# Attention slots of a decoder step: unit work ahead of the sample's work, and an earlier start of the first product

## The reference, cut to what matters

```python
z = rmsnorm(x, norm1_g) @ w_in            # q, three K/V pairs, gates, pooling input
# prompt and sample each: compressed, selected-block and window attention, merged by gates
o = g0 * o_cmp + g1 * o_sel + g2 * o_win
h = x + concat(o, pool_mix(u)) @ w_out
y = h + peer_ffn(rmsnorm(h, norm2_g))     # product-key search, single-neuron experts
```

## Time and profile before

| | us |
|---|---|
| median of three runs | 1768.33 |
| the profiled execution's own time | 1764.12 |
| its span on the core | 1762.4 |
| around the span | 1.7 |
| TensorE busy in the span | 1682.8 (95%) |
| VectorE / ScalarE / GpSimd busy | 1369.0 / 739.3 / 457.6 |
| project, attend, all later stages | 0 to 162, 162 to 397, 398 to 1762 |

### The profile page before, as it was taken

The page is one execution under the profiler, slowest core; times in us unless marked ns, Lnnn a source line. Parts: engine busy times, 40 slices in busy tenths (PEclk is TensorE's granted clock), DMA queues, the critical chain, the costliest instruction groups (busy, mean ns, idle before and its releaser), DMA issues.

```text
span 1762.4 us, 29599 instructions
## 1 busy us (share of the span) xinstructions
PE 1682.8 (95%) x10384; PEld 1590.3 (90%) x10384; DVE 1369.0 (78%) x2809; ACT 739.3 (42%) x1392; POOL 457.6 (26%) x375
## 2 busy tenths in 40 slices
PE   7997988789999899999999999999999999999999
PEld 5876775559999899999999999999999899999999
DVE  3065335655578899999998998886898899999996
ACT  1023235434321433466665667863333333333333
POOL 0001100001100023333223225443344444444440
PEclk9898989789999999999999999999999999999999
DMA  9224412323322478988999889999899999999994
GB/s 305 66 62 154 128 44 67 88 64 96 108 70 64 138 273 293 328 294 316 313 323 318 311 286 371 365 367 385 309 382 381 367 403 395 400 397 391 396 393 165
DMA packets 196759, 457.31 MB, mean 259 GB/s; under 512 B 25842, under 2 KB 102898, under 8 KB 196146
## 3 DMA queue, kind: packets, MB, share of 16 engines
q1 hardware_dynamic: 123154, 252.34, 40.9%
q0 software_dynamic: 47440, 175.54, 26.8%
q10 hardware_dynamic: 26016, 27.53, 4.5%
HBM read 402.71 MB, written 56.05 MB: 260 GB/s over the span
## 4 chain that ended last, share of the span: by engine, by line
PE 60%; DVE 4%; DMA 1%; issue 1%; ACT 0%; SPq 0%; DVEq 0%; ACTq 0%; POOLq 0%
PE ps L1884 9%; PE ps L1881 9%; PE ps L1880 9%; PE ps L1908 9%; PE ps L1911 9%; PE ps L1914 9%; PE ps L1930 5%; DVE sb_w_lo L1713 1%; DMA sb_ring<-expert_v 1%; DVE sb_slot L1750 0%; DMA sb_expert_row<-expert_v,sb_row_expert 0%; DVE sb_rows_y L1843 0%; DVE sb_hot L1749 0%; ACT sb_w_hi L1617 0%; DVE sb_hot L1746 0%
## 5 line engine op out<-in xcount | busy, mean ns | idle before, releaser
L1617 ACT ACTIVATE sb_w_hi<-sb_ring 128x1024 fp32r<-128x1024 f32 x256 | 271.5, 1061 | 512.5 <-PE ps L1914 228.9
L1713 DVE TENSOR_TENSOR sb_w_lo<-sb_ring,sb_w_hi 128x1024 fp32r<-128x1024 f32 x256 | 313.5, 1225 | 65.2 <-ACT sb_w_hi L1617 57.8
L1880 PE MATMUL ps<-sb_x_hi,sb_w_hi 128*128 128x384 f32 x1024 | 351.5, 343 | 6.0 <-ACT sb_w_hi L1617 4.4
L1881 PE MATMUL ps<-sb_x_lo,sb_w_hi 128*128 128x384 f32 x1024 | 346.7, 339 | 0.0
L1884 PE MATMUL ps<-sb_x_hi,sb_w_lo 128*128 128x384 f32 x1024 | 201.9, 338 | 5.4 <-DVE sb_w_lo L1713 5.4
L1908 PE MATMUL ps<-sb_x_lo,sb_w_hi 128*128 128x384 f32 x1016 | 197.5, 336 | 4.8 <-ACT sb_x_lo L1626 4.8
L1880 PEld LDWEIGHTS ps<-sb_x_hi,sb_w_hi 128*128 128x128 f32 x1024 | 192.7, 188 | 6.6 <-ACT sb_w_hi L1617 6.6
L1914 PE MATMUL ps<-sb_x_lo,sb_w_hi 128*128 128x384 f32 x1016 | 197.1, 335 | 0.0
L1911 PE MATMUL ps<-sb_x_lo,sb_w_lo 128*128 128x384 f32 x1016 | 197.1, 335 | 0.0
L1881 PEld LDWEIGHTS ps<-sb_x_lo,sb_w_hi 128*128 128x128 f32 x1024 | 193.1, 189 | 0.0
L1884 PEld LDWEIGHTS ps<-sb_x_hi,sb_w_lo 128*128 128x128 f32 x1024 | 181.5, 187 | 7.7 <-DVE sb_w_lo L1713 7.7
(11 more groups left out here) (329 smaller groups left out, 2510.1 us busy)
## 6 DMA issues: line engine op xcount, KB each, us to landing
sb_ring<-expert_u SPq DMA_DIRECT2D x128, 512.0 KB
sb_ring<-expert_v SPq DMA_DIRECT2D x128, 512.0 KB
gates_dense<-sb_g_stage ACTq DMA_DIRECT2D x12, 2048.0 KB
hid_dense<-sb_hid SPq DMA_DIRECT2D x112, 192.0 KB
sb_scores<-hid_dense SPq DMA_DIRECT2D x112, 192.0 KB
sb_g_stage<-gates_dense SPq DMA_DIRECT2D x32, 384.0 KB
sb_g_stage<-gates_dense SPq DMA_DIRECT2D x48, 256.0 KB
sb_ring<-peer_wq SPq DMA_DIRECT2D x16, 512.0 KB
```

The lines of the kernel that those rows point to most:

```text
L1617: nc.scalar.activation(whi[v % 2][:, :], ring(v)[:, :], ACT.Copy).then_inc(w_hi, 1)
L1713: nc.vector.tensor_tensor(wlo[v % 2][:, :], ring(v)[:, :], whi[v % 2][:, :], ALU.subtract).then_inc(w_lo, 1)
L1880: nc.tensor.matmul(out, hi[:, c * P:(c + 1) * P], g.x_hi[:, c], start=(c == 0), stop=False)
L1881: nc.tensor.matmul(out, hi[:, c * P:(c + 1) * P], g.x_lo[:, c], start=False, stop=False)
```

## The change

In `project`, norm1 is loaded by SyncE ahead of x and counts into `x_in[0]`, which the readers of x chunks 0 and 1 now await at 32. `first_in` counts only `c_mean_d` and `c_eps`; VectorE's wait for it before the first product and TensorE's first wait are gone, and the later ones ask for 32.

In `attend`, TensorE does turn(s-2) and values(s-3) right behind scores(s), and the compressed-branch turn and all sample work behind them. ScalarE does the gelu and the row groups' exponentials, then the unit's copies, then the copies and roots that follow a product of the same slot; the copy `so` moves from slot +8 to +7. VectorE adds the parts of a `sub` product one slot later, and `key_norm` comes one slot later.

```diff
@@ sync, project
+            sp.dma_start(norm1[:, :], g.a["norm1"]).then_inc(x_in[0], 16)
             for k in range(4):
@@ tensor, project
-            pe.wait_ge(first_in, 48)
...
-            pe.wait_ge(first_in, 48)
+            pe.wait_ge(first_in, 32)
@@ scalar, project
-            act.dma_start(norm1[:, :], g.a["norm1"]).then_inc(first_in, 16)
@@ scalar and vector, project, in the loop over k
-                act.wait_ge(x_in[k // 2], 16)
+                act.wait_ge(x_in[k // 2], 16 if k >= 2 else 32)
@@ vector, project
-            dve.wait_ge(first_in, 48)
@@ tensor, attend, in slot s
                 if s < NU_ATT:
                     scores(s)
+                if 0 <= s - 2 < NU_ATT:
+                    turn(s - 2)
+                if 0 <= s - 3 < NU_ATT:
+                    values(s - 3)
                 if ("turn", s) in cmp_at:
                     cmp_turn(cmp_at["turn", s])
...
-                if 0 <= s - 2 < NU_ATT:
-                    turn(s - 2)
-                if 0 <= s - 3 < NU_ATT:
-                    values(s - 3)
@@ scalar, attend, in slot s: order after the change
 exp(s); gelu; row exponentials; first_turned(s - 2); compressed-branch copy; put_out(s - 3);
 sub copy; square and value copy; root; so copy (now s == b + 7); row_turn copies
@@ vector, attend, in slot s
+                if s - 1 in SUB_SLOTS:
+                    add_parts(SUB_SLOTS.index(s - 1))
...
-                if s in SUB_SLOTS:
-                    add_parts(SUB_SLOTS.index(s))
...
-                    if s == SUB_SLOTS[4 * e + 3] + 3:
+                    if s == SUB_SLOTS[4 * e + 3] + 4:
                         key_norm(e)
```

More of the change, by code:

```diff
@@ L394, in _ @@
                 nc.scalar.activation(sq[:, square_at(k)], g.xT[:, k], ACT.Square).then_inc(sq_ready, 1)
-            act.wait_ge(first_in, 48)
+            act.wait_ge(first_in, 32)
             act.wait_ge(sq_used, KC)
@@ L500, in add_square @@
                 nc.vector.tensor_tensor(sq[:, 0], sq[:, 0], sq[:, square_at(k)], ALU.add).then_inc(sq_used, 1)
-            dve.wait_ge(first_in, 48)
             for k in range(KC):
-                dve.wait_ge(x_in[k // 2], 16)
+                dve.wait_ge(x_in[k // 2], 16 if k >= 2 else 32)
                 nc.vector.tensor_scalar(xg[:, k], g.xT[:, k], norm1[:, k:k + 1], None, ALU.mult).then_inc(xg_ready, 1)
@@ L885, in _ @@
                     exp(s)
+                for e in range(2):
+                    if s == SUB_SLOTS[4 * e + 3] + 1:
+                        act.wait_ge(summed, 4 * e + 4)
+                        nc.scalar.activation(hS[:, :, :, :, :].rearrange("p c g b n -> p (c g) b n"), h0[:, :, :, 0:NCMP_S], ACT.Gelu_apprx_tanh).then_inc(gelu, 1)
+                for bt, b in enumerate(ROW_SLOTS):
+                    if s == b + 2:
+                        act.wait_ge(s_bias, bt + 1)
+                        nc.scalar.activation(sc, sc, ACT.Exp, bias=snm[:, 0:1], scale=g.c["c_slope_s"][:, :], accum_out=srs[:, 0:1])
+                        nc.scalar.activation(sw, sw, ACT.Exp, bias=snm[:, 2:3], scale=g.c["c_slope_s"][:, :], accum_out=srs[:, 2:3]).then_inc(s_exp, 1)
+                    if s == b + 4:
+                        act.wait_ge(s_bias_sel, bt + 1)
+                        nc.scalar.activation(ss, ss, ACT.Exp, bias=snm[:, 1:2], scale=g.c["c_slope_s"][:, :], accum_out=srs[:, 1:2]).then_inc(s_exp_sel, 1)
+                if 0 <= s - 2 < NU_ATT:
+                    first_turned(s - 2)
+                if ("turn", s) in cmp_at:
+                    j = cmp_at["turn", s]
+                    act.wait_ge(g.z_stored, 32)
+                    act.wait_ge(c_turn, j + 1)
+                    nc.scalar.activation(ptc[:, j], bank(g, 5)[:, 256:512], ACT.Copy).then_inc(c_out, 1)
+                if 0 <= s - 3 < NU_ATT:
+                    put_out(s - 3)
                 if s in SUB_SLOTS:
@@ L891, in _ @@
                 for e in range(2):
-                    if s == SUB_SLOTS[4 * e + 3] + 1:
-                        act.wait_ge(summed, 4 * e + 4)
-                        nc.scalar.activation(hS[:, :, :, :, :].rearrange("p c g b n -> p (c g) b n"), h0[:, :, :, 0:NCMP_S], ACT.Gelu_apprx_tanh).then_inc(gelu, 1)
                     if s == SUB_SLOTS[4 * e + 3] + 2:
@@ L903, in _ @@
                 for bt, b in enumerate(ROW_SLOTS):
[L904 to L911, removed]
+                    if s == b + 7:
                         act.wait_ge(so_mm, bt + 1)
@@ L917, in _ @@
                         nc.scalar.activation(pt_[:, 8 * part:8 * part + 4], bank(g, 6).rearrange("p (k n) -> p k n", k=4), ACT.Copy).then_inc(s_t_act, 1)
[L918 to L926, removed]
         @block.vector
```

## The result

The changed kernel takes 1778.6 us (median of 14 runs), the kernel before 1771.6 in as many runs beside it; the ratio is 1.0046, 95% interval 1.0031 to 1.006. One run of each kernel, at 2383.7 us (granted clock 0.648 against 0.97 in the others) and at 2777.4 us, was a disturbed one and is left out of the ratio. The forecast was 1769.6, "same", 1.3 above the three runs of before. The change cost 7.0 instead, a slowdown of just under the half per cent that was named as the bound of what can be told; 1778.6 is also past the range's upper end of 1775. Of the 9.0 between forecast and result, 3.3 is the kernel before, which has a median of 1771.6 in 14 runs and had 1768.3 in three; 5.7 is the change. The profiled executions lie further apart than the medians: 1774.1 us after (span 1772.4) against 1764.1 before (span 1762.4), +10.0.

A forecast was written before the change was run, and what follows sets the result against it. TensorE was taken as the bound, 60% of the chain that ended last; +5.6 at the start and -4.3 in attention gave +1.3 on 1768.3, so 1769.6 us, "same", range 1758 to 1775.

The forecast's parts named there:

- Part 1: In `project`: first product 6.1 us earlier, but weight tile 3 late behind the 4 MB copy; +5.6 us, ends -0.7 and +8.5.
- part 2: In `attend`: the new order saves 2.6 up to the eighth `sub` and 1.7 behind line 801; -4.3 us, ends -1.0 and -7.2.
- It stands behind SyncE's own list of constants, to which norm1 adds 0.4, so 28.6.: In `project`: SyncE issues weight tile 3 at 28.6 us instead of 28.21, however early TensorE starts.
- SyncE's queue came free 44 - 30.74 = 13.3 after the copy's issue, so at 37.9 now.: In `project`: the queue, free at 37.9, moves tile 3 in 3.0 us; it lands at 41, and TensorE idles for 9.4.
- The part's high end: In `project`: tile 3 lands at 43.9, 19.3 after the copy's issue, making the start's term +8.5 us.
- The 39.5: In `project`: tile 3's landing if queues strictly take turns by packet, with the start's term +4.1 instead of +5.6 us.
- The eighth `sub` 2.6 earlier.: In `attend`: the eighth `sub` product, where the queue's chain starts, comes 2.6 us earlier, ends 0.9 and 4.1.
- The wait at line 762 grown to 6 or more.: In `attend`: a sign of being right, TensorE's wait there for a load growing from 3.12 to 6 us or more.
- Does TensorE reach line 801 in time? It fits, with 2 to spare; this margin is what would be lost first.: In `attend`: TensorE gets from line 762 to line 801 before SyncE's last values, with 2 us to spare.
- Tile 3 is not held up: Rival in `project`: tile 3 slips past the copy, the start's term is -6.1, kernel 1757.9 us; chance 0.18.
- Clock lost: Rival in `project`: clock stays at 1.2 GHz through the fourth item, start's term +13.6, kernel 1777.6 us; chance 0.09.
- reorder without effect: Rival in `attend`: `key_mean` holds `key_norm`, the eighth `sub` gains nothing, attention gains 1.7 or less, kernel 1772.2 us; chance 0.21.

The follow-up runs named there:

- norm1_act: The changed kernel with the load of norm1 put first in ScalarE's queue, still counted with x; 1782.4 us in one run.
- copy_late: The changed kernel with GpSimd's 4 MB copy issued after four items instead of two; 1770.0 us against 1770.3, ratio 0.9989.
- slots_copy_first: The kernel before with only the new attention order, and ScalarE's first unit copy ahead of the gelu and exponentials; 1773.1 us against 1772.9, ratio 0.9991.
- start_only: The kernel before with only the edits in `project` (norm1 ahead of x, no wait for the epsilon); 1782.7 us against 1770.3, ratio 1.0074.
- slots_only: The kernel before with only the new slot order in `attend`; 1770.8 us, ratio 0.9992.
- copy_early: The kernel before with the 4 MB copy issued after one item instead of two; 1787.7 us, ratio 1.0077.
- best_b: The changed kernel, tile 3 issued ahead of SyncE's constants, ScalarE's first unit copy ahead of gelu and exponentials, 4 MB copy after four items; 1762.5 us, ratio 0.9961.

## Why the prediction was wrong

Part 1's mechanism was the one forecast, the copy ahead of tile 3; the tile's landing was mis-sized by 6.1 us. In part 2 two steps failed. Between the +1.3 of the forecast and the +10.0 of the profiles lie 8.7: 4.2 from part 1, 3.0 from part 2 and 1.5 from the stages behind attention.

- **The start.** Right: first product at 6.91 (6.4 forecast, low end 5.9, high end 7.6), released by VectorE, VectorE by x. The first item took 9.33 (9.65), the copy went out at 25.42 (24.6).
- **"It stands behind SyncE's own list of constants, to which norm1 adds 0.4, so 28.6."** 30.80 measured. `norm1_act` shows that the added issue is not most of it; 1.2 of the delay comes before the copy, and later single issues stall (c_gate_row 1.56).
- **"SyncE's queue came free 44 - 30.74 = 13.3 after the copy's issue, so at 37.9 now. At the rate of rows 8 ... its 0.52 MB take 3.0: 41."** This is the step that failed. The tile landed at 47.1, and 43.9 had been the high end. The 6.1 have two parts.
  - The queue came free at about 40 and not at 37.9: from 38 to 40 us it moved 0.01 MB. The 44 of the prediction was where the window of the earlier trace rows ends. In the kernel before the queue moved only 0.12 MB from 44 to 46 us too; it picked up at 46, which is 15 after that copy's issue as well. The earlier trace rows had it: the copy lands after 15.8.
  - The tile did not have the queue to itself. By the sizes of SyncE's loads, those ahead of tile 3 are 7.70 MB, and the queue had moved 7.41 at 40: 0.29 of constants were left, and with the tile's 0.52 that is 0.81 MB. At the 0.28 MB/us of 40 to 47 us this is 2.9 us, as forecast, and the tile would have landed at 43. But by 47.1 the queue had moved 9.38 MB, and everything up to and including tile 5, issued at 40.0, is 9.28. So the last piece of tile 3 landed when tiles 4 and 5, issued behind it, had moved too. That is an account by bytes; no run issues tiles 4 and 5 later to test it.
  - The part's high end failed for the same reasons: it took the time at which the queue was empty before, when tile 3 and the constants were no longer in it. In copy-free `copy_late` the same issue lands in 4.4. The wait was 14.7 instead of 9.4, and the fourth item ended at 56.5 instead of 50.7: +5.8.
- **One thing was left out in the other direction.** A shift was to pass behind the fourth item one for one. The one-column products took 9.39 instead of 11.34, at a granted clock of 0.75 instead of 0.61, so +11.4 became +9.8 at attention's start. Part 1 is thus +9.8 against +5.6 forecast and +8.5 as its worst.
- The page "DMA: Bandwidth & Descriptors" of the Trainium skill, section "Queues, rings and completion order", has each DMA engine take turns between the queues with work, a packet at a time. The trace agrees: 45 packets against 45 from 31 to 39 us. The prediction set this aside because of 25 against 51 in the earlier trace rows. In that trace it is 19 against 19 from 34 to 38 us, and then 1 against 27 from 38 to 42, although SyncE had issued tile 5 at 37.8; why nothing of it moved until 42 stays open. The 39.5 that it drew from the rule was further off than its own 41, because it took the tile to move in these turns, and what stood ahead of it in the queue were packets of a few hundred bytes.
- **"The eighth `sub` 2.6 earlier."** 283.01 - 172.85 = 110.2 from attention's start, against 111.2: 1.0 earlier, near the low end of 0.9, and not even that repeats: the other kernels with this order, ScalarE's aside, have 110.1 to 117.6, the ones with the old order 110.7 to 112.7. The prediction had turn(5) run in the gelu's shadow and asked only what values(4) waits for. But that turn itself waited, 3.69 at 232.96, where the earlier trace rows have 3.22 for the gelu: it needs ScalarE's copy behind the gelu, and row weights of VectorE that were no earlier. The shadow stayed empty. The 3.69 is the same in all five kernels with this order.
- **"The wait at line 762 grown to 6 or more."** 4.60. Four waits ahead of it, between 289 and 332 us, for ScalarE's copy (2.80, 1.32, 2.19) and a row maximum (2.52), took 8.8 of TensorE's time. `slots_copy_first` brings those on the copy down, and the wait at that line becomes 8.95.
- **"Does TensorE reach line 801 in time? It fits, with 2 to spare; this margin is what would be lost first."** It did not fit. From line 759 to line 798 it is 38.6 (37.4 before), and TensorE reaches it without waiting, 399.17 against a last issue that ended at 361.65 + 34.46 = 396.1. The prediction had asked that `cache_sel_v` still release it. With the 1.2 lost there, 1.6 less gained ahead of the eighth `sub` and 0.3 lost ahead of line 759, part 2 is -1.3 instead of -4.3. As attention's length differs by more than that between profiles, only the next step is firm.
- Behind line 798 it was 8.0 instead of 9.8: -1.8, as forecast (-1.7), and 8.0 in every kernel with the new order.
- **The rivals.** "Tile 3 is not held up" is refuted by the three kernels that issue it behind the copy (the changed one, `start_only`, `norm1_act`). "Clock lost", at 1777.6, came nearest to the 1778.6, for the wrong reason: the clock was low for the fourth item's first 3 us and not throughout, and it took 9.37, what the forecast had priced (9.65). The rest of the miss went into the landing. For part 2, "reorder without effect" is nearest: `slots_only` is at 0.9992. But it gave `key_mean` as the cause, and that is not where the waits are: they stand at the unit's turn, for ScalarE's copy and VectorE's row weights.

The sum with the measured terms is +9.8 - 1.3 + 1.5 = +10.0, and by the medians +7.0. The stages behind attention were taken to pass the shift unchanged; they took 1.5 more, with the granted clock at 0.99. `start_only` lost 12.4 by its medians and 13.3 in its profile: 8.7 at attention's start, -0.3 in attention, and 5.0 in the later stages, which no edit touches. Why those differ between executions, by up to 13 us, was not looked into; where a total differs from the sum of its parts by a few us, this is the first place to look.

## What to carry to other kernels

Before work is pulled forward, list the transfers that its end triggers and the ones that the next steps want, in the order in which they will now be issued: here an earlier second item let a 4 MB copy pass one weight tile of 0.5 MB, and 5.6 us won became 9.8 lost. A load stuck behind such a copy is priced from the copy's landing on, and not by its own size but by all that stands in its queue then, what was issued behind it included. And where several engines wait in turn for one chain, removing stalls off that chain buys nothing: shorten the chain, here by letting a second engine issue half the pages, which took the ratio from 0.9961 to 0.9906.

## What the runs showed of the hardware

- A DRAM-to-DRAM copy of 4064 KB went in packets of 65 KB (59 for 3.84 MB). While it ran, another queue got one packet for each of its packets (45 and 45 from 31 to 39 us; 34 and 34 in `start_only`, 46 and 46 in `copy_early`), or fewer (1 and 27 before the change, from 38 to 42); with packets of a few hundred bytes 45 were 0.01 MB. The engine that owns the queue can be stopped too: one issue of SyncE's took 7.69 in `copy_early`, and its list came to tile 3 at 37.9 instead of 28.2.
- A weight tile of 0.52 MB behind that copy landed 16.3 after its issue, when the two tiles issued behind it had moved as well; without the copy it took 4.4.
- An item's matmuls (x32) take 7.39 in a running block, and 9.2 to 10.3 as the first block after a pause, of 3.2 us (9.24), 6.9 (10.31), 13.0 (9.24 and 9.59) and 14.7 (9.37): the price of a restart does not grow with the pause here.
- The same one-column products (x64) took 8.9 us in `best_b` and 11.6 in `copy_early`, at a mean granted clock of 0.79 and 0.60: time and clock multiply to 6.9 in both.
